# A two-block transformer step on one core: weights laid out on the host in load order, one 16 KB run per partition

## The reference

```python
        sh1, sc1, g1, sh2, sc2, g2 = [m[:, None, :] for m in adaln(c, w_mod[l], b_mod[l])]
        hx = modulate(rmsnorm(x, norm1_g[l]), sh1, sc1)
        hc = modulate(rmsnorm(cs, norm1_g[l]), csh1, csc1)
        qa, ka, va, qb, kb, vb = split_proj(hx @ w_in[l])      # w_in 1024 x 2304
...
    def expert_block(args):
        tok, e = args
        xb = x_pad[tok]
        h = xb @ w_gu[e] + b_gu[e]                             # w_gate_up 32 x 1024 x 2048
        g = jnp.minimum(h[:, ::2], SWIGLU_LIMIT)
        lin = jnp.clip(h[:, 1::2], -SWIGLU_LIMIT, SWIGLU_LIMIT)
        a = g * jax.nn.sigmoid(SWIGLU_ALPHA * g) * (lin + 1.0)
        return a @ w_dn[e] + b_dn[e]                           # w_down 32 x 1024 x 1024
...
        proj = h @ w_in[l]                                     # second block, 1024 x 5888
...
        u = causal_depthwise_conv(h @ w_ffn_up[l], ffn_conv_w[l], ffn_conv_b[l])
        y = (jax.nn.gelu(u_gate, approximate=True) * u_val) @ w_ffn_down[l]
```

## Time and profile before

| | us |
|---|---|
| median of 3 runs | 1743.92 |
| lowest and highest run | 1742.03, 1745.68 |
| span of the profiled execution | 1743.0 |
| PE busy | 1597.5 (92%) |
| DVE busy | 544.6 (31%) |
| ACT busy | 444.3 (25%) |
| bytes read from HBM | 522.72 MB, 301 GB/s over the span |

### The profile page before, as it was taken

One profiled execution on the slowest core, in us unless ns is written; L12 is line 12 of the kernel. 1 busy time (PEld: TensorE's weight loads), 2 busy tenths in 40 slices (PEclk: granted clock), 3 DMA queues, 4 the chain that ended last, 5 costly groups with the idle time before them and its releaser, 6 DMA issues.

```text
span 1743.0 us, 24227 instructions
## 1 busy us (share of the span) xinstructions
PE 1597.5 (92%) x10048; PEld 995.3 (57%) x10048; DVE 544.6 (31%) x1092; ACT 444.3 (25%) x856; POOL 7.3 (0%) x16
## 2 busy tenths in 40 slices
PE   4999899999999998989999899999789989899997
PEld 2786676434443443333333334333389988889997
DVE  3754513101010101010100101010255564468763
ACT  3434523101010101010010101000345553345642
POOL 0000000000000000000000000000000100000000
PEclk9999998999999999999999999999999989989999
DMA  9425953999999999999999999999925523525430
GB/s 361 165 92 209 325 182 138 420 416 419 416 420 417 418 418 417 418 417 419 416 420 416 418 418 418 419 417 418 377 74 193 182 96 105 183 100 173 172 116 25
DMA packets 127525, 524.75 MB, mean 301 GB/s; under 512 B 4467, under 2 KB 12659, under 8 KB 94276
## 3 DMA queue, kind: packets, MB, share of 16 engines
q1 hardware_dynamic: 124464, 519.06, 75.2%
q10 hardware_dynamic: 2484, 3.19, 0.7%
q0 software_dynamic: 512, 1.57, 0.4%
HBM read 522.72 MB, written 1.08 MB: 301 GB/s over the span
## 4 chain that ended last, share of the span: by engine, by line
PE 74%; DMA 16%; DVE 5%; ACT 4%; issue 1%; SPq 0%; ACTq 0%; DVEq 0%
PE ps L573 72%; DMA ring<-in_w_gate_up 14%; ACT arena L1319 1%; PE ps L899 1%; DMA ring<-in_w_in 1%; ACT arena L1335 1%; DMA arena<-in_ctxT 1%; DVE mx L1631 1%; PE ps L1009 0%; ACT arena L1250 0%; DVE arena L1533 0%; PE ps L701 0%; PE ps L888 0%; DVE nrm L1530 0%; ACT w_high L1356 0%
## 5 line engine op out<-in xcount | busy, mean ns | idle before, releaser
L573 PE MATMUL ps<-ring,arena 128*64 128x512 f32 (+1 forms) x3872 | 716.2, 534 | 42.5 <-ACT arena L1335 24.4
L573 PEld LDWEIGHTS ps<-ring,arena 128*64 128x64 f32 (+1 forms) x3872 | 250.2, 133 | 481.6 <-issue 443.8
L573 PE MATMUL ps<-arena_r,w_high 128*128 128x256 f32 x1840 | 340.9, 288 | 10.2 <-DVE arena_r L1834 9.4
L573 PEld LDWEIGHTS ps<-arena_r,w_high 128*128 128x128 f32 x1840 | 291.1, 194 | 15.1 <-issue 12.8
L573 PE MATMUL ps<-arena 64*128 64x256 f32 (+7 forms) x1812 | 267.4, 379 | 15.6 <-ACT arena L1319 11.7
L573 PE MATMUL ps<-arena_r,ring_r 128*128 128x256 f32 x920 | 262.4, 285 | 0.0
L1773 DVE TENSOR_SCALAR arena<-ps 128x512 f32<-128x512 f32 x32 | 22.1, 692 | 768.1 <-PE ps L573 768.1
L573 PEld LDWEIGHTS ps<-arena 64*128 64x128 f32 (+4 forms) x1812 | 173.4, 178 | 99.2 <-issue 74.5
L573 PEld LDWEIGHTS ps<-arena_r,ring_r 128*128 128x128 f32 x920 | 178.9, 194 | 0.0
L1808 DVE TENSOR_TENSOR ring_r<-ring,w_high 128x1024 fp32r<-128x1024 f32 x120 | 141.9, 1220 | 86.3 <-ACT w_high L1356 86.3
L1328 ACT ACTIVATE arena<-arena 128x512 f32<-128x512 f32 x32 | 20.2, 630 | 518.5 <-DVE arena L1773 518.5
(11 more groups left out here) (205 smaller groups left out, 1011.2 us busy)
## 6 DMA issues: line engine op xcount, KB each, us to landing
ring<-in_w_gate_up SPq DMA_DIRECT2D x128, 2048.0 KB, 21.9
ring<-in_w_down SPq DMA_DIRECT2D x64, 2048.0 KB, 19.9
ring<-in_w_in SPq DMA_DIRECT2D x15, 2048.0 KB, 15.6
ring<-in_w_mod SPq DMA_DIRECT2D x12, 2048.0 KB, 9.0
ring<-in_w_ffn_up SPq DMA_DIRECT2D x11, 2048.0 KB, 8.0
ring<-in_w_ffn_down SPq DMA_DIRECT2D x5, 2048.0 KB, 7.7
ring<-in_w_out SPq DMA_DIRECT2D x4, 2048.0 KB, 9.2
ring<-in_w_in SPq DMA_DIRECT2D x2, 1024.0 KB, 5.3
```

The costliest lines, as they stand in the source:

```text
L573: return nc.tensor.matmul(out_, lhsT, rhs, start=start, stop=stop, **kw)
```

## The change

The host writes two flat arrays, `first` and `second`, in which the units stand in the order in which they are loaded, each as 128 partitions x 4096 values, and gives w_gate_up and w_down the shapes 32 x 4 x 128 x 4096 and 32 x 2 x 128 x 4096. A partition's share of a unit is then one run of 16 KB in HBM (8 KB for the four half-size units). The bytes in each slot, their places in SBUF, the sizes of the DMAs, their order, their waits and all work of the other engines stay as they are. The host does its layout before the launch.

```diff
-        def blocks(w, c0, width):
-
-            return w.rearrange("(k p) n -> p k n", p=P)[:, :, c0:c0 + width]
-
-        def rows(w, k0, nk):
-
-            return w.rearrange("(k p) n -> p k n", p=P)[:, k0:k0 + nk, :]
...
+        def units(stream, plan):
+
+            at, out_ = 0, []
+            for _, _, _, n_ in plan:
+                out_.append(io[stream][at:at + P * n_].rearrange("(p n) -> p n", p=P))
+                at += P * n_
+            return out_
+
+        w_gu, w_dn = io["w_gate_up"], io["w_down"]
+        first, second = units("first", FIRST), units("second", SECOND)
...
         def unit_dst(index, src):
-            n = 1
-            for s in src.shape[1:]:
-                n *= s
-            return ring[:, index, 0:n].rearrange("p (k n) -> p k n", k=src.shape[1])
+            return ring[:, index, 0:src.shape[1]]
...
-            gu_rows = w_gu.rearrange("e (k p) n -> e p k n", p=P)
-            dn_rows = w_dn.rearrange("e (k p) n -> e p k n", p=P)
-
             def expert_unit(e, q):
-                if q < 4:
-                    return slot(SLOT_MOE[q], 2), gu_rows[e, :, 2 * q:2 * q + 2, :]
-                return slot(SLOT_MOE[q], 4), dn_rows[e, :, 4 * (q - 4):4 * (q - 4) + 4, :]
+                return ring[:, SLOT_MOE[q], :], w_gu[e, q] if q < 4 else w_dn[e, q - 4]
...
+def laid_out(plan, weights):
+
+    flat = []
+    for name, at, width, n in plan:
+        w = weights[name].reshape(-1, P, weights[name].shape[-1])
+        part = w[at:at + n // D] if width is None else w[:, :, at:at + width]
+        flat.append(part.transpose(1, 0, 2).reshape(-1))
+    return np.concatenate(flat)
```

More of the change, by code:

```diff
@@ L91, with blocks, rows @@
 ARENA = 25088
+def blocks(name, c0, width):
+    return name, c0, width, KC * width
+def rows(name, k0, nk):
+    return name, k0, None, nk * D
+FIRST = [blocks("w_mod", 512 * u, 512) for u in range(4)]
+U_IN = len(FIRST)
+FIRST += [blocks("w_in", 512 * u, 512) for u in range(4)] + [blocks("w_in", 2048, 256)]
+U_KV = len(FIRST)
+FIRST += [blocks("w_mem_kv_2", 0, 256), blocks("w_mem_kv_2", 512, 512)]
+U_MOD2 = len(FIRST)
+FIRST += [blocks("w_mod", 512 * u, 512) for u in range(4, 12)]
+U_OUT = len(FIRST)
+FIRST += [blocks("w_out", 512 * u, 512) for u in range(2)]
+U_KV2 = len(FIRST)
+FIRST += [blocks("w_mem_kv_2", 256, 256)]
+U_MOE = len(FIRST)
+V_IN = 0
+SECOND = [blocks("w_in_2", c0, 512) for c0 in (0, 512, 1024, 2304, 1536)] + [blocks("w_in_2", 2048, 256)]
+SECOND += [blocks("w_in_2", 2816 + 512 * u, 512) for u in range(6)]
+V_BR = len(SECOND)
+SECOND += [rows(n, 0, 4) for n in ("w_branch_moba_2", "w_branch_swa_2", "w_branch_mem_2")]
+V_OUT = len(SECOND)
+SECOND += [blocks("w_out_2", 512 * u, 512) for u in range(2)]
+V_UP = len(SECOND)
+SECOND += [blocks("w_ffn_up_2", 512 * u, 512) for u in range(FC // 2)]
+V_DN = len(SECOND)
+SECOND += [rows("w_ffn_down_2", 4 * u, min(4, FC - 4 * u)) for u in range((FC + 3) // 4)]
 def build(nc, io, out):
@@ L282, in build @@
         MORE.units, MORE.units0, MORE.full, MORE.full0 = more_units, 1, more_full, lambda q: 16
-        def blocks(w, c0, width):
-            return w.rearrange("(k p) n -> p k n", p=P)[:, :, c0:c0 + width]
-        def rows(w, k0, nk):
-            return w.rearrange("(k p) n -> p k n", p=P)[:, k0:k0 + nk, :]
-        w_mod, w_in, w_out = io["w_mod"][0], io["w_in"][0], io["w_out"][0]
-        w_in2, w_kv, w_out2 = io["w_in_2"][0], io["w_mem_kv_2"][0], io["w_out_2"][0]
-        w_up, w_down2 = io["w_ffn_up_2"][0], io["w_ffn_down_2"][0]
@@ L2027, in shape_constants @@
     return {a: np.ascontiguousarray(b, dtype=f) for a, b in out.items()}, onehot
-_BIG = ["w_mod", "w_in", "w_out", "w_gate_up", "w_down", "b_gate_up", "b_down", "w_in_2", "w_mem_kv_2",
-        "w_branch_moba_2", "w_branch_swa_2", "w_branch_mem_2", "w_out_2", "w_ffn_up_2", "w_ffn_down_2"]
+def laid_out(plan, weights):
[5 more added lines that the diff above has]
+    return np.concatenate(flat)
 def kernel(**inputs):
@@ L2056 @@
     }
-    for n in _BIG:
-        arrays[n] = x[n]
-    arrays["w_ffn_up_2"] = x["w_ffn_up_2"].reshape(1, D, 2, FC // 2, 2 * P).transpose(0, 1, 3, 2, 4).reshape(1, D, -1)
+    weights = {n: x[n][0] for n in ("w_mod", "w_in", "w_out", "w_in_2", "w_mem_kv_2", "w_branch_moba_2", "w_branch_swa_2",
+                                    "w_branch_mem_2", "w_out_2", "w_ffn_down_2")}
+    weights["w_ffn_up_2"] = x["w_ffn_up_2"].reshape(D, 2, FC // 2, 2 * P).transpose(0, 2, 1, 3).reshape(D, -1)
+    arrays["first"], arrays["second"] = laid_out(FIRST, weights), laid_out(SECOND, weights)
+    arrays["b_gate_up"], arrays["b_down"] = x["b_gate_up"], x["b_down"]
+    arrays["w_gate_up"] = x["w_gate_up"][0].reshape(N_EXPERTS, 4, 2, P, -1).transpose(0, 1, 3, 2, 4).reshape(N_EXPERTS, 4, P, SLOT)
+    arrays["w_down"] = x["w_down"][0].reshape(N_EXPERTS, 2, 4, P, -1).transpose(0, 1, 3, 2, 4).reshape(N_EXPERTS, 2, P, SLOT)
     nc = bacc.Bacc("TRN2", target_bir_lowering=False, num_devices=1)
```

## The result

| | us |
|---|---|
| before, median of 4 runs | 1743.68 |
| changed, median of 4 runs | 1722.51 |
| changed, lowest and highest | 1720.73, 1723.09 |
| ratio, with its 95% interval | 0.9875, 0.9861 to 0.9889 |

The change makes the kernel 21.2 us faster (1.2%). The prediction was 1722.3. The profiled execution of the changed kernel has a span of 1718.9 us, which is 24.1 less than that of before. In all runs the device time is 1.8 us more than the span; so the changed kernel's profiled execution (1720.73) is 1.8 us faster than its median, and that of before (1743.0 + 1.8) is 1.1 us slower than its median of 1743.68. These 2.9 us of the 24.1 are the spread of runs.

The account below looks back on a forecast made before the run. PE was taken as the bound, with expert loads slightly slower and stalling it. 1743.0 - 19.0 (expert stalls) - 2.6 (start) = 1721.4, plus 0.9 to the median: 1722.3 us; range 1718 to 1732 with the 15% rival, 1719 to 1725 without.

Parts of the forecast that it names:

- The bound: Expert loop: loads (60.2 us a pair) race PE (58.33); late loads cost PE 19.0 us, in the second half.
- The cost of a run: All load units: each run costs a DMA engine 9.8 ns, so a 16 KB unit takes 4.87 us (4.88 used).
- PE's cap: Expert loop: PE's pace limits the gain to 19.0 us of stalls, not 24.5 of loading; last load 5.6 ahead.
- The start: Before the experts: the first w_in unit lands earlier, gaining 2.6 us, between 2.0 (if modcol decides) and 2.7.
- The rest: Eight later w_mod units, w_out and the second block: loaded ahead of use, hidden behind PE, gain 0.
- A: All units: longer runs bring less, perhaps cut at 8 KB; 4.95 us a unit, some stalls stay, 1730.5 us; 15%.
- B (flat): All loads: the rates differ by something other than runs, so nothing is gained, 1744 us; 5%.
- C: All loads: engines reading 16 KB apart meet in one part of memory, slower, 1817 us at 387 GB/s; 7%.
- Signs: Changed kernel's trace, if right: 35,000 to 40,000 packets, experts at 429 to 431 GB/s, no PE wait for w_gate_up.

Follow-up runs that it names:

- The kernel of 8 KB runs: Changed kernel, but each expert unit gives a partition two runs of 8 KB within one contiguous 2 MB block; 1732.20 us.
- the second block alone: Kernel before, with only the second block's units laid out as one run for a partition; 1743.80 us, ratio 1.0005.

## Why the prediction was right

**The bound.** Reading the slices and the few waits as a race of two nearly equal rates was right. The 19.0 us from the timeline (17.1 up to expert 31's bias, 1.9 in it) came back to the tenth. One reading was loose: the stalls were put in the second half of the loop. PE's first wait for w_gate_up ends at 683.87 us, after six of the fifteen pairs, so they fill the last nine pairs; the sum doesn't use it.

**The cost of a run.** 9.8 ns was a little high: the expert windows of 10 and 20 us gave 423 and 424 GB/s for 8 KB, where 850 us of nothing but such runs give 422. The landings show 9.4 to 9.5 ns at every step. A 16 KB unit takes 4.89 us, not 4.87 to 4.88.

**PE's cap.** It made the gain insensitive to that error, but narrowly. The 5.6 us of lead that I had worked out at expert 31 were 2.2 us: in the trace its fourth unit lands at 1201.21, and PE comes to it at 1193.03 + 10.4 = 1203.4. So the full 19.0 hung on a margin smaller than I thought. The kernel of 8 KB runs, 0.07 us a unit slower, already stalls 17 times.

**The start.** 2.6 us in the trace (40.17 to 37.54, 59.93 to 57.31). One detail was wrong without effect: modcol's last part came at 35.38, not 36.5. PE's 64 multiplications with the last w_mod unit took 1.96 us instead of 2.98: its wait for that unit shrank from 2.87 to 1.05 us, and the granted clock was still 1.00 (2.4 GHz) from 32 to 36 us, when it now did them; before, after the longer wait, it was 0.50 (1.2 GHz) from 36 to 44. DVE then waited 1.79 us for ACT's part of the w_in unit, so the unit decides, as predicted.

**The rest.** Zero was right: 1.0005 for the second block alone.

**Rivals.** A was real in kind, though not for 16 KB: had the packets been cut at 8 KB, it would have been 1732.2, where the prediction worked out 1730.5. B (flat) fell with every length. C had a basis: a layout with neighbours 2 MB (and 1 MB for w_down) apart would have been slower than before (1777). That the engines meet in one part of the memory fits it but is not shown; at the 16 KB of this change, and at 32 and 64 KB, there is no loss.

**Signs.** I had expected 35,000 to 40,000 packets, and it is 41,253: the loads outside the change are 9,509 packets, where that forecast leaves 3,300 to 8,300 beside the 31,744. No term rested on it.

Left open: the 2.5 us by which the two profiled spans differ beyond start and experts. Repeated traces show such differences without the change, but nothing names their cause.

## What to carry to other kernels

Where loads are the bound, count the runs (contiguous pieces) for each DMA engine: here each cost 9.4 ns beside the bytes, so 2 KB runs gave 387 GB/s and 16 KB runs 428. Price the gain against the engine that takes over: of 23 us less loading (0.76 us for each of 30 experts by the landings, and four units), 19.0 arrived, since PE's own pace was 3% away. When laying weights out for long runs, don't put the partitions' runs exactly 2 MB from each other: with the w_gate_up units laid out so, the rate fell by 6%, and 4 KB more in the distance gave it back.

## What the runs showed of the hardware that I had not expected

The cost of a run is the same from 1 to 16 KB, 9.4 to 9.5 ns at every step, and it doesn't matter whether the runs of a unit lie in one contiguous block or a matrix row apart. Runs of 16 KB are moved as single packets (41,253 in all). With partitions exactly 2 MB from each other for w_gate_up and 1 MB for w_down, the loads run at 404 instead of 428 GB/s, unevenly (364 and 436 in two windows of 10 us). Three of the four units at 2 MB take 5.35 to 5.58 us instead of 4.89, those at 1 MB don't suffer, and 4 KB of padding removes the loss.
